# Two more buffers for split weights, five units kept for the second tile, and an aligned start of the large buffers

## The chip, the cores and the metric

The kernel runs on one core of one Trainium2 chip. The time is the device time of one execution in microseconds (us). The engines are TensorE (PE in the profile; its loads of the stationary operand are PEld), VectorE (DVE), ScalarE (ACT), GpSimd (POOL) and SyncE (SP), which issues the transfers of weights.

## The reference, cut to what matters

Two transformer blocks follow one another on 256 rows of 1024 float32 numbers. The first has a block attention and a gated delta rule, a gated merge, an output product, a gated feed-forward layer of width 2816 and a small embedding with a gate. The second has a differential attention, pooling, an output product, cross attention over a memory of 256 rows, and a feed-forward layer. After each large product the row is normalised, added to the residual and normalised again before the next product:

```
h = h + rms_norm(merged @ w_out, ln_post_mix)
f = rms_norm(h, ln_pre_ffn)
f = (silu(f @ w_ffn_gate) * (f @ w_ffn_up)) @ w_ffn_down
h = h + rms_norm(f, ln_post_ffn)
h = h + sigmoid(h @ w_ple_gate) * rms_norm(p @ w_ple, ln_ple)
...
x = x + rms_norm(mix @ w_out_2, g_mix_post)
xq = rms_norm(x, g_x_pre) @ w_xq
x = x + rms_norm(softmax(xq k') v @ w_xo, g_x_post)
x = x + rms_norm(ffn(rms_norm(x, g_ffn_pre)), g_ffn_post)
```

## The kernel before, in words

**Weights.** All weights are cut into 294 units of 128 x 1024 numbers (`UNITS`), in the order in which TensorE uses them. Each unit goes through three stages in this order: SyncE brings it into one of `RAW` = 4 raw slots; ScalarE rounds it to the high part `w_hi` (L1213, one copy of 128x1024); GpSimd computes the low part `w_lo` = raw - high (L470, two halves). High and low part stand in slot n % `SPLIT` of `SPLIT` = 6. A raw slot is free when the low part of its unit is there; a split slot is free when TensorE has counted the unit in `w_used`. A product with the split activations (`uH`, `uL` and others) is a triple of matmuls (`split_mm`, L481 to L483): high by high, high by low, low by high. The activation is the stationary operand and the weights move past it, except in `conv` (L829 to L831) and `keys` (L740 to L742), where the weights are stationary and 256 columns of activations move.

**Queues.** Each engine runs one list of instructions in order. ScalarE's list mixes the copies of weights with the work of the stages: `split_up_to(n)` emits the copies of all units below n at that place, and each waits for its transfer and for the release of its slot. `split_past(step, j)` is `split_up_to(NUMBER[step, j] + 1 + SPLIT)`, so its last copy waits for the release of unit j of that step. Whatever ScalarE has behind such a copy waits with it.

**Row products.** `proj_b`, `w_out`, `ple_gate`, `xq` and `xo` have eight units each and are written by `skewed_rows`, `out2` and `down` by `row_unit` and `row_tail`. A unit has four pieces (row tile t = 0 or 1, column half c = 0 or 1), each one triple into its own PSUM bank `L[2t+c]`. Row tile 0 runs ahead of tile 1: the last `TAIL` = 4 units are first used for tile 0 and then for tile 1, so that the normalisation of tile 0 runs beside the last pieces of tile 1. In `skewed_rows` the units 2 and 3 of tile 1 stand before the last three units of tile 0.

**Between two products** (ScalarE `norm` and `next`, the same on VectorE): ScalarE sums the squares of a bank (`row_sum`, L1300); VectorE multiplies by a gain (L1835), takes the root (seven small operations, L1768), adds the residual (L1853) and scales (`hg`, L1864); TensorE turns four blocks (`turn_half`, L686); ScalarE rounds them to `uH` (`hi_half`, L1225); VectorE computes `uL` (L1801). This goes by quarters, (t, half) = (0,0), (0,1), (1,0), (1,1). `following` puts the turn of (0,0) before the very last piece of a product. VectorE's list has `uL` of quarter (0,1) ahead of the root and sum for tile 1. ScalarE's has two copies of weights between the quarters (0,1) and (1,0), and the sum of squares of the whole row tile 1 (`square_sum`, L1289) before `uH` of (1,1).

**Column products** after such a junction (`ffn` 0 of both blocks and `in2` 0 and 1) are written by `skewed_columns`: for tile 0 four units of the first matrix and two of the second, then the same six units for tile 1, then the last two units of the second for both tiles. For tile 1 the third unit waits for `uL` of quarter (1,1).

**Cross attention.** ScalarE copies the last values to `xv` (`values_out`, L1244) after `split_past(("xkv", 3), 3)`, and TensorE's `cross_values` (L804) reads them.

**Memory.** The buffers are placed one after another from `base`. `w_hi`, `w_lo`, `uH` and `uL` start at multiples of 512 bytes from `base`; `Y`, where `yH`, `yL`, `hH` and `hL` stand, starts at such a multiple plus 32, and so do `B` = Y + 16 KB and all that is placed from it (`mH`, `mL`, `pH` and the buffers of attention and norms).

Of the kernel before, what the change touches and what calls it, by code (L numbers as in the profile page):

```python
# [22 lines left out]
F32 = mybir.dt.float32  # L23
F32R = mybir.dt.float32r
# [22 lines left out]
RAW, SPLIT = 4, 6  # L47
UNIT = 1024
KB = 1024
MAGIC = 1.5 * 2.0 ** 23  # L50
# [109 lines left out]
HEAD = 5  # L160
TAIL = 4

# [56 lines left out]
def build(nc, a, out, known):  # L219
# [7 lines left out]
    for n, (step, j, _) in enumerate(UNITS):  # L227
        FIRST.setdefault(step, n)
        LAST[step] = n
        NUMBER[step, j] = n  # L230
    ctx = ExitStack()
    with ctx:
# [101 lines left out]
        cp = big("cp", 16, [P, NT, GH, SEQ])  # L334
        cpT = place("cpT", [P, NT, GH, SEQ], F32, Y)
        used = B + 100 * KB
        assert used <= nc.sbuf_usable_end, (used, nc.sbuf_usable_end)
# [126 lines left out]
        @block.gpsimd  # L464
        def _(pool):
            for n in range(len(UNITS)):
                pool.wait_ge(w_hi_there, n + 1)
                for half in range(2):
                    cc = slice(half * UNIT // 2, (half + 1) * UNIT // 2)
                    last = nc.gpsimd.tensor_tensor(w_lo[:, n % SPLIT, cc], raw[:, n % RAW, cc], w_hi[:, n % SPLIT, cc].bitcast(F32),  # L470
                                                   ALU.subtract)
                last.then_inc(w_lo_there, 1)
# [3 lines left out]
        def _(pe):  # L476
# [8 lines left out]
            def unit(n, k):  # L485
                slot = n % SPLIT
                return (w_hi[:, slot, :].rearrange("p (k n) -> p k n", k=k),
                        w_lo[:, slot, :].rearrange("p (k n) -> p k n", k=k))

            def column_unit(step, j, banks, n=512, sH=uH, sL=uL, tiles=range(NT), ks=None):  # L490

# [19 lines left out]
                if 1 in tiles and per - 1 in ks:  # L511
                    last.then_inc(w_used, 1)
                elif 1 not in tiles and k == k_tiles - 1:
                    last.then_inc(*PE.mark(step, "first tile"))
# [60 lines left out]
            def skewed_rows(step):  # L575
# [38 lines left out]
            def skewed_columns(first, second, first_banks, second_banks):  # L614


                source = INPUT[first[0]]
                for t in range(NT):
                    wait_low(source, t, 0)
                    bank_free(source, t, 0)  # L620
                    for j in range(4):
                        if j == 1:
                            turn_half(source, t, 1)
                        elif j == 2:
                            wait_low(source, t, 1)
                        column_unit(first[0], first[1] + j, first_banks, tiles=(t,))
                    bank_free(source, t, 1)
                    for j in range(2):
                        if t == 0 and j == 1:
                            turn_half(source, 1, 0)  # L630
                        column_unit(second[0], second[1] + j, second_banks, tiles=(t,))
                for j in range(2, 4):
                    column_unit(second[0], second[1] + j, second_banks)
# [55 lines left out]
            def wait_low(source, t, half):  # L689

                pe.wait_ge(*VE(source, "lo", t, half))
# [152 lines left out]
            for step in SCHEDULE:  # L844
# [328 lines left out]
                elif kind == "dnorm":  # L1173
# [7 lines left out]
                    pe.wait_ge(*AC(("xkv", 1), 1))  # L1181
                    for j in range(4):
                        row_unit(("out2",), j, uH, uL, KD)
# [18 lines left out]
        def _(act):  # L1202
# [24 lines left out]
            def split_past(step, j):  # L1227


                split_up_to(NUMBER[step, j] + 1 + SPLIT)  # L1230

# [105 lines left out]
            def fill(step, i):  # L1337

                split_up_to(FIRST[FILLING[step][0]] + i + SPLIT)

# [4 lines left out]
            for step in SCHEDULE:  # L1345
# [3 lines left out]
                if kind in ("ba", "rates", "tri", "conv", "decay", "moba", "tok", "feat", "within", "att", "inv", "scan", "z", "ga", "gb"):  # L1349
                    split_up_to(consumed + SPLIT - 1)  # L1350
                if kind == "u":
# [16 lines left out]
                elif kind == "rates":  # L1368
                    split_up_to(consumed + SPLIT + 1)
                    act.wait_ge(*VE(step, "ba"))  # L1370
# [156 lines left out]
                elif kind == "down":  # L1527
                    prev = ("ffn", step[1], 5)
                    if step[1] == 1:
                        split_past(step, 2)  # L1530
                        act.wait_ge(landed["lnm"], 16)
                        for j in range(4):
# [20 lines left out]
                elif kind == "norm":  # L1553
# [6 lines left out]
                    if what == "ffn2":  # L1560
                        row_sum(what, 2)
                        row_sum(what, 3)
                        continue
                    split_past(src_step, last - 3)
                    if pre:
                        kept(what, 0, 0)
                elif kind == "next":
# [15 lines left out]
                    if pre:  # L1583
                        kept(what, 1, 1)
                        square_sum(what, 1)
                    hi_half(step, 1, 1)
                elif kind == "ffn":
                    _, blk, c = step
                    n = 512 if c < 5 else 256
                    half = (LAST[step] + 1 - FIRST[step]) // 2  # L1590
                    split_up_to(FIRST[step] + half + SPLIT - 1)
                    act.wait_ge(*fed(step, half))
# [11 lines left out]
                    for c_ in todo:  # L1604
                        prev = ("ffn", blk, c_)
                        if c_ == 5:
                            split_up_to(FIRST[("down", blk)] + SPLIT)
                        elif (blk, c) == (1, 1):
# [11 lines left out]
                    split_up_to(consumed + SPLIT - 1)  # L1620
                elif kind == "in2":
# [724 lines left out]
```

## Time and profile before

| | |
|---|---|
| median of 3 runs | 1018.12 us (1018.11 to 1018.43) |
| profiled execution | 1018.06 us, span of the instructions 1016.2 us |
| TensorE busy | 982.5 us (97%), granted clock 1.0 of full speed in every slice |
| GpSimd busy | 741.5 us (73%), 588 halves of low parts, 1300 ns each |
| ScalarE busy | 513.1 us (50%), 304.9 us of it the 294 copies of weights |
| VectorE busy | 366.5 us (36%) |
| DMA | 165 GB/s in the mean |

TensorE is nearly always busy, so the profile is read in two ways: how far apart matmuls of one shape start, and where TensorE has an idle gap and what ended it. Busy times of matmuls overlap (one starts while the one before drains), so the distance of two starts is the cost, not the busy time.

### The profile page before, as it was taken

Reading aid. Unit: us, or ns where it says so; the run is one execution under the profiler, and the core shown is the slowest. Engines: PE = TensorE matmul, PEld = TensorE weight load, DVE = VectorE, ACT = ScalarE, POOL = GpSimd, SP = SyncE. Lnnn points to the kernel's source line nnn. Section 1 sums busy time; section 2 is a strip of 40 time slices with the busy share of each in tenths; the row PEclk is TensorE's granted clock in tenths of the full one; section 3 lists DMA queues with packets and bytes.
Section 4 is the critical chain, followed back from the end, with each engine's and each line's share of the span. In section 5 each row is a group of like instructions: output and inputs, shape, how many; then the busy total and the mean of one; then the engine's idle time right before and its main releaser. Section 6 shows DMA issues by size and latency. Waiting matters only on the chain.

```text
span 1016.2 us, 15323 instructions
## 1 busy us (share of the span) xinstructions
PE 982.5 (97%) x6004; PEld 826.8 (81%) x6004; DVE 366.5 (36%) x840; ACT 513.1 (50%) x759; POOL 741.5 (73%) x592
## 2 busy tenths in 40 slices
PE   5999999999999998999999998999989999999997
PEld 5988889988888876888898876899868868888885
DVE  4677524686524135112122244243242161111103
ACT  5476624464524435465454455485465365444431
POOL 6767643877633876989986966878767469988891
PEclk9999999999999999999999999999999999999999
DMA  8546232554423665667764645655555247766551
GB/s 263 175 133 194 90 120 64 167 159 152 126 85 103 212 202 166 207 202 208 208 186 145 197 149 172 240 167 168 164 170 162 83 144 228 207 188 188 185 166 41
DMA packets 76752, 167.37 MB, mean 165 GB/s; under 512 B 8348, under 2 KB 13704, under 8 KB 76552
## 3 DMA queue, kind: packets, MB, share of 16 engines
q1 hardware_dynamic: 71296, 156.40, 49.9%
q10 hardware_dynamic: 5384, 9.99, 3.0%
q8 instruction: 47, 0.77, 0.3%
q14 instruction: 25, 0.20, 0.1%
HBM read 165.32 MB, written 1.05 MB: 164 GB/s over the span
## 4 chain that ended last, share of the span: by engine, by line
PE 86%; DVE 4%; ACT 4%; POOL 3%; issue 2%; DMA 0%; DVEq 0%; ACTq 0%
PE L L481 20%; PE L L483 19%; PE L L482 19%; POOL w_lo L470 3%; PE L L829 2%; PE L L830 2%; PE L L831 2%; PE Q L481 2%; PE Q L483 2%; PE Q L482 2%; PE Q L998 1%; ACT w_hi L1213 1%; PE Q L980 1%; PE Q L686 1%; ACT uH L1225 1%
## 5 line engine op out<-in xcount | busy, mean ns | idle before, releaser
L470 POOL TENSOR_TENSOR w_lo<-raw,w_hi 128x512 fp32r<-128x512 f32 x588 | 741.3, 1300 | 254.1 <-ACT w_hi L1213 253.5
L1213 ACT CAST w_hi<-raw 128x1024 fp32r<-128x1024 f32 x294 | 304.9, 1054 | 262.4 <-PE L L483 118.8
L481 PE MATMUL L<-w_hi,uH 128*128 128x512 f32 (+1 forms) x768 | 306.9, 400 | 12.8 <-POOL w_lo L470 4.8
L483 PE MATMUL L<-w_hi,uL 128*128 128x512 f32 (+1 forms) x768 | 296.5, 386 | 0.0
L482 PE MATMUL L<-w_lo,uH 128*128 128x512 f32 (+1 forms) x768 | 296.1, 386 | 0.0
L481 PEld LDWEIGHTS L<-w_hi,uH 128*128 128x128 f32 x768 | 144.4, 188 | 52.2 <-DVE uL L1801 9.9
L483 PEld LDWEIGHTS L<-w_hi,uL 128*128 128x128 f32 x768 | 144.3, 188 | 29.8
L482 PEld LDWEIGHTS L<-w_lo,uH 128*128 128x128 f32 x768 | 144.6, 188 | 26.1 <-issue 0.5
L481 PE MATMUL L<-w_hi,hH 128*128 128x512 f32 x176 | 70.0, 398 | 0.0
L482 PE MATMUL L<-w_lo,hH 128*128 128x512 f32 x176 | 69.6, 395 | 0.0
L483 PE MATMUL L<-w_hi,hL 128*128 128x512 f32 x176 | 69.6, 395 | 0.0
L1762 DVE TENSOR_TENSOR hL<-Q,hH 128x512 fp32r<-128x512 f32 x22 | 15.2, 692 | 121.3 <-ACT hH L1619 120.8
L829 PE MATMUL L<-uH,w_hi 128*128 128x256 f32 x192 | 55.5, 289 | 0.0
L830 PE MATMUL L<-uL,w_hi 128*128 128x256 f32 x192 | 54.9, 286 | 0.0
L831 PE MATMUL L<-uH,w_lo 128*128 128x256 f32 x192 | 54.8, 286 | 0.0
L1835 DVE TENSOR_TENSOR L<-L,gA 128x512 f32<-128x512 f32 x20 | 14.0, 700 | 103.5 <-ACT hg L1300 103.0
L1768 DVE TENSOR_SCALAR small<-small 128x1 f32<-128x1 f32 (+1 forms) x177 | 39.0, 220 | 24.3 <-ACT xv L1544 13.4
L1801 DVE TENSOR_TENSOR uL<-Q,uH 128x512 fp32r<-128x512 f32 x28 | 19.3, 691 | 58.4 <-ACT uH L1225 58.4
L483 PEld LDWEIGHTS L<-w_hi,hL 128*128 128x128 f32 x176 | 33.1, 188 | 8.0
L482 PEld LDWEIGHTS L<-w_lo,hH 128*128 128x128 f32 x176 | 33.1, 188 | 7.7
L481 PEld LDWEIGHTS L<-w_hi,hH 128*128 128x128 f32 x176 | 33.1, 188 | 7.7
L1771 DVE SCALAR_TENSOR_TENSOR hm<-L,small,sil 128x512 f32<-128x512 f32 x20 | 15.0, 751 | 66.6 <-PE L L483 66.2
(335 smaller groups left out, 1283.2 us busy)
## 6 DMA issues: line engine op xcount, KB each, us to landing
raw<-in_w_in SPq DMA_DIRECT2D x88, 512.0 KB, 3.6
raw<-in_w_ffn_gate SPq DMA_DIRECT2D x22, 512.0 KB, 3.6
raw<-in_w_ffn_up SPq DMA_DIRECT2D x22, 512.0 KB, 3.7
raw<-in_w_ffn_down SPq DMA_DIRECT2D x22, 512.0 KB, 3.5
raw<-in_w_gate SPq DMA_DIRECT2D x22, 512.0 KB, 4.2
raw<-in_w_up SPq DMA_DIRECT2D x22, 512.0 KB, 4.1
raw<-in_w_down SPq DMA_DIRECT2D x22, 512.0 KB, 3.5
raw<-in_w_out SPq DMA_DIRECT2D x16, 512.0 KB, 3.6
```

The source lines that it names most:

```text
L470: last = nc.gpsimd.tensor_tensor(w_lo[:, n % SPLIT, cc], raw[:, n % RAW, cc], w_hi[:, n % SPLIT, cc].bitcast(F32), ALU.subtract)
L481: mm(dst, sH, wH, start=start, stop=False)
L482: mm(dst, sH, wL, start=False, stop=False)
L483: return mm(dst, sL, wH, start=False, stop=stop)
L829: mm(bank, sH, uH[:, k, :], start=k == 0, stop=False)
L830: mm(bank, sH, uL[:, k, :], start=False, stop=False)
L831: last = mm(bank, sL, uH[:, k, :], start=False, stop=k == KD - 1)
L1213: copy(w_hi[:, u % SPLIT, :], raw[:, u % RAW, :]).then_inc(w_hi_there, 1)
L1762: v(V.tensor_tensor(out_, x_, y_, op), *name)
L1768: v(V.tensor_scalar(out_, x_, s1, s2_, op0, op1), *name)
L1771: v(V.scalar_tensor_tensor(out=out_, in0=x_, scalar=s_, in1=y_, op0=op0, op1=op1), *name)
L1801: vector_next(V.tensor_tensor(uL[:, 4 * half:4 * half + 4, t * P:(t + 1) * P], heads(Q[2 * t + half]), uH[:, 4 * half:4 * half + 4, t * P: ...
```

## The change

(a) Six further slots of split weights lie in memory that is free for a time; two of them are open in each of four stretches (`SCAN`: from unit 7 of `proj_a` to `ffn` 1,4; `GATE`: from unit 19 of `down` 1 to `in2` 2; `OUT`: from unit 6 of `out2` to `ffn` 2,0; `MEMORY`: from unit 4 of `xo` to the end). `SLOT` and `BEFORE` say for each unit its slot and the unit that had it before; the copy waits for `w_used` of that one. `room(used)` is the number of units that may be split once `used` units are used: 8 ahead in the stretches, up to 10 around `xo`, 6 elsewhere. All `split_*` calls use it in place of `+ SPLIT`.
(b) `TAIL` is 5: unit 3 of a row product (unit 17 of `down`) is held for tile 1 too. In `skewed_rows` only unit 2 of tile 1 stands in the middle.
(c) In `skewed_rows` the turn of quarter (0,1) stands after the third piece and not after the first.
(d) `skewed_columns` takes for tile 1 two units of the first matrix, two of the second, and then the last two of the first; the wait for quarter (1,1) stands before these.
(e) ScalarE makes `uH` of (1,1) before `square_sum` of tile 1.
(f) `Y` starts at a multiple of 512 bytes from `base`.

```diff
-TAIL = 4
+TAIL = 5
+    LENT = {SPLIT: (SCAN, MEMORY), SPLIT + 1: (SCAN, MEMORY), SPLIT + 2: (GATE,), SPLIT + 3: (GATE,), SPLIT + 4: (OUT,), SPLIT + 5: (OUT,)}
...
+        slot = min(free_slots, key=lambda s: newest.get(s, -1))
+        SLOT.append(slot)
+        BEFORE.append(newest.get(slot, -1))
...
+    def room(used):
+        n = 0
+        while n < len(UNITS) and BEFORE[n] < used:
+            n += 1
+        return n
...
+        at[0] += (base - at[0]) % SPAN
         Y = at[0]
...
-                    if j == 0 and source[0] == "next":
+                    if j == 2 and source[0] == "next":
                         turn_half(source, 0, 1)
...
-                for j in (2, 3):
+                for j in range(2, KD - TAIL):
...
+                wait_low(source, 1, 0)
+                bank_free(source, 1, 0)
+                column_unit(first[0], first[1], first_banks, tiles=(1,))
+                turn_half(source, 1, 1)
+                column_unit(first[0], first[1] + 1, first_banks, tiles=(1,))
+                bank_free(source, 1, 1)
+                for j in range(2):
+                    column_unit(second[0], second[1] + j, second_banks, tiles=(1,), used=0)
+                wait_low(source, 1, 1)
+                column_unit(first[0], first[1] + 2, first_banks, tiles=(1,))
+                column_unit(first[0], first[1] + 3, first_banks, tiles=(1,), used=3)
...
-                    if u >= SPLIT:
-                        act.wait_ge(w_used, u - SPLIT + 1)
-                    copy(w_hi[:, u % SPLIT, :], raw[:, u % RAW, :]).then_inc(w_hi_there, 1)
+                    if BEFORE[u] >= 0:
+                        act.wait_ge(w_used, BEFORE[u] + 1)
...
+                    copy(halves[SLOT[u]][0], raw[:, u % RAW, :]).then_inc(w_hi_there, 1)
...
-                split_up_to(NUMBER[step, j] + 1 + SPLIT)
+                split_up_to(room(NUMBER[step, j] + 1))
...
-                    split_past(src_step, last - 3)
+                    split_past(src_step, last - TAIL + 1)
...
+                    hi_half(step, 1, 1)
+                    if pre:
                         square_sum(what, 1)
-                    hi_half(step, 1, 1)
```

The calls `split_past(step, 3)` in `w_out`, `ple_gate`, `out2`, `xq` and `xo` are as before.

## Rows read from the trace of the kernel before

**Rows 1.** Page, part 1: busy us (share of the span) x instructions.
```profile
PE 982.5 (97%) x6004; PEld 826.8 (81%) x6004; DVE 366.5 (36%) x840; ACT 513.1 (50%) x759; POOL 741.5 (73%) x592
```

**Rows 2.** Waits of PE, whole span: waiter, releaser: us in total, times, longest.
```profile
PE L L481 <- POOL w_lo L470: 4.8, 11, 0.8
PE L L481 <- DVE uL L1801: 4.2, 6, 0.8
...
PE L L481 <- DVE small L1768: 2.6, 3, 1.0
```

**Rows 3.** Timeline of PE in `ffn` 2,2: start us, duration, instruction.
```profile
879.69 0.39 PE L482 MATMUL L<-w_lo,uH 128*128 128x512 f32 x1
...
885.58 0.39 PE L481 MATMUL L<-w_hi,uH 128*128 128x512 f32 x1
```

**Rows 4.** Timeline of PE in `down` 2.
```profile
959.72 0.40 PE L481 MATMUL L<-w_hi,hH 128*128 128x512 f32 x1
...
965.55 0.40 PE L482 MATMUL L<-w_lo,hH 128*128 128x512 f32 x1
```

**Rows 5.** Groups by line and form, PE: xcount | busy us, mean ns | idle before.
```profile
L481 PE MATMUL L<-w_hi,hH 128*128 128x512 f32 x176 | 70.0, 398 | 0.0
...
L481 PE MATMUL Q<-w_hi,mH 128*128 128x512 f32 x32 | 13.1, 409 | 0.0
L481 PE MATMUL L<-w_hi,yH 128*128 128x512 f32 x32 | 12.9, 403 | 0.0
```

**Rows 6.** Timeline of PE in the first `conv`.
```profile
17.54 0.28 PE L829 MATMUL L<-uH,w_hi 128*128 128x256 f32 x1
...
19.94 0.28 PE L831 MATMUL L<-uH,w_lo 128*128 128x256 f32 x1
```

**Rows 7.** Timeline of PE in `keys` of the memory.
```profile
674.72 0.28 PE L741 MATMUL L<-mL,w_hi 128*128 128x256 f32 x1
...
677.76 0.28 PE L740 MATMUL L<-mH,w_hi 128*128 128x256 f32 x1
```

**Rows 8.** Timeline of PE, end of `w_out`; in brackets idle before and its releaser.
```profile
381.51 0.40 PE L483 MATMUL L<-w_hi,uL 128*128 128x512 f32 x1
382.72 0.50 PE L481 MATMUL L<-w_hi,uH 128*128 128x512 f32 x1 [0.82 <-POOL w_lo L470]
...
388.98 0.60 PE L686 MATMUL Q<-table,hg 128*128 128x128 f32 x4
...
391.05 0.50 PE L481 MATMUL L<-w_hi,uH 128*128 128x512 f32 x1 [0.78 <-DVE uL L1801]
```

**Rows 9.** Timeline of ACT, end of `w_out`.
```profile
376.52 3.89 ACT L1213 CAST w_hi<-raw 128x1024 fp32r<-128x1024 f32 x4
383.72 0.60 ACT L1300 ACTIVATE hg<-L 128x512 f32<-128x512 f32 x1 [3.31 <-PE L L483]
```

**Rows 10.** Timeline of DVE, end of `w_out`.
```profile
387.87 0.69 DVE L1864 TENSOR_TENSOR hg<-L,gB 128x512 f32<-128x512 f32 x1
```

**Rows 11.** Timeline of POOL in `w_out`.
```profile
377.65 8.77 POOL L470 TENSOR_TENSOR w_lo<-raw,w_hi 128x512 fp32r<-128x512 f32 x7 [6.17 <-ACT w_hi L1213]
```

**Rows 12.** Timeline of ACT and of PE in `ffn` 1,0, tile 1.
```profile
403.50 1.06 ACT L1289 ACTIVATE tmp<-h 128x1024 f32<-128x1024 f32 x1
...
405.98 0.50 PE L481 MATMUL L<-w_hi,uH 128*128 128x512 f32 x1 [0.78 <-DVE small L1768]
```

**Rows 13.** Timeline of DVE in `ple_gate`.
```profile
593.34 0.69 DVE L1801 TENSOR_TENSOR uL<-Q,uH 128x512 fp32r<-128x512 f32 x1 [0.79 <-ACT uH L1225]
...
595.75 0.75 DVE L1853 SCALAR_TENSOR_TENSOR h<-L,small,h 128x512 f32<-128x512 f32 x1
```

**Rows 14.** Timeline of ACT and of PE in the cross attention.
```profile
786.59 1.07 ACT L1244 COPY xv<-Q 128x512 f32<-128x512 f32 x2
...
787.71 2.05 PE L804 MATMUL Q<-cpT,xv 128*128 128x128 f32 x16 [0.38 <-ACT xv L1244]
```

**Rows 15.** DMA issues by line: KB each, median us to landing.
```profile
gB<-in_g_mix_pre ACTq DMA_DIRECT2D x1, 512.0 KB, 3.7
```

More of the change, by code:

```diff
@@ L48 @@
 UNIT = 1024
+SPAN = 512
 KB = 1024
@@ L230, in build @@
         NUMBER[step, j] = n
+    SCAN, GATE, OUT, MEMORY = range(4)
+    OPENED = {SCAN: NUMBER[("proj_a",), 7], GATE: NUMBER[("down", 1), 19], OUT: NUMBER[("out2",), 6], MEMORY: NUMBER[("xo",), 4]}
+    CLOSED = {SCAN: LAST["ffn", 1, 4], GATE: LAST["in2", 2], OUT: LAST["ffn", 2, 0], MEMORY: len(UNITS) - 1}
+    LENT = {SPLIT: (SCAN, MEMORY), SPLIT + 1: (SCAN, MEMORY), SPLIT + 2: (GATE,), SPLIT + 3: (GATE,), SPLIT + 4: (OUT,), SPLIT + 5: (OUT,)}
+    SLOT, BEFORE = [], []
+    newest = {}
+    for n in range(len(UNITS)):
+        if n == OPENED[MEMORY]:
+            newest.update({s: LAST["xkv", 3] for s, whens in LENT.items() if MEMORY in whens})
+        free_slots = list(range(SPLIT)) + [s for s, whens in LENT.items() if any(OPENED[o] <= n <= CLOSED[o] for o in whens)]
+        slot = min(free_slots, key=lambda s: newest.get(s, -1))
+        SLOT.append(slot)
+        BEFORE.append(newest.get(slot, -1))
+        newest[slot] = n
+    ENTRY = {n: o for o in (SCAN, GATE, OUT) for n in [next(n for n in range(OPENED[o], len(UNITS)) if SLOT[n] >= SPLIT)]}
+    def room(used):
[3 more added lines that the diff above has]
+        return n
     ctx = ExitStack()
@@ L335, in build @@
         cpT = place("cpT", [P, NT, GH, SEQ], F32, Y)
+        lent = {SPLIT: (84, 88), SPLIT + 1: (92, 96), SPLIT + 2: (68, 72), SPLIT + 3: (76, 80), SPLIT + 4: (60, 64), SPLIT + 5: (-8, -4)}
+        halves = {n: (w_hi[:, n, :], w_lo[:, n, :]) for n in range(SPLIT)}
+        for n, (hi_at, lo_at) in lent.items():
+            halves[n] = (big(f"w_hi{n}", hi_at, [P, UNIT], F32R)[:], big(f"w_lo{n}", lo_at, [P, UNIT], F32R)[:])
         used = B + 100 * KB
@@ L469, in _ @@
                     cc = slice(half * UNIT // 2, (half + 1) * UNIT // 2)
-                    last = nc.gpsimd.tensor_tensor(w_lo[:, n % SPLIT, cc], raw[:, n % RAW, cc], w_hi[:, n % SPLIT, cc].bitcast(F32),
-                                                   ALU.subtract)
+                    hi, lo = halves[SLOT[n]]
+                    last = nc.gpsimd.tensor_tensor(lo[:, cc], raw[:, n % RAW, cc], hi[:, cc].bitcast(F32), ALU.subtract)
                 last.then_inc(w_lo_there, 1)
@@ L485, in unit, with column_unit @@
             def unit(n, k):
[L486 to L490, printed above, removed]
+                hi, lo = halves[SLOT[n]]
+                return hi.rearrange("p (k n) -> p k n", k=k), lo.rearrange("p (k n) -> p k n", k=k)
+            def column_unit(step, j, banks, n=512, sH=uH, sL=uL, tiles=range(NT), ks=None, used=1):
                 n0 = NUMBER[step, j]
@@ L511, in column_unit @@
                 if 1 in tiles and per - 1 in ks:
-                    last.then_inc(w_used, 1)
+                    if used:
+                        last.then_inc(w_used, used)
                 elif 1 not in tiles and k == k_tiles - 1:
@@ L617, in skewed_columns @@
                 source = INPUT[first[0]]
[L618 to L631, printed above, removed]
+                wait_low(source, 0, 0)
+                bank_free(source, 0, 0)
+                for j in range(4):
+                    if j == 1:
+                        turn_half(source, 0, 1)
+                    elif j == 2:
+                        wait_low(source, 0, 1)
+                    column_unit(first[0], first[1] + j, first_banks, tiles=(0,))
+                bank_free(source, 0, 1)
+                column_unit(second[0], second[1], second_banks, tiles=(0,))
+                turn_half(source, 1, 0)
+                column_unit(second[0], second[1] + 1, second_banks, tiles=(0,))
+                wait_low(source, 1, 0)
[9 more added lines that the diff above has]
+                column_unit(first[0], first[1] + 3, first_banks, tiles=(1,), used=3)
                 for j in range(2, 4):
@@ L1181, in _ @@
                     pe.wait_ge(*AC(("xkv", 1), 1))
-                    for j in range(4):
+                    for j in range(KD - TAIL):
                         row_unit(("out2",), j, uH, uL, KD)
@@ L1337, in fill @@
             def fill(step, i):
-                split_up_to(FIRST[FILLING[step][0]] + i + SPLIT)
+                split_up_to(room(FIRST[FILLING[step][0]] + i))
             load("ident", table[:, 0:P], a["table"][:, 0:P])
@@ L1590, in _ @@
                     half = (LAST[step] + 1 - FIRST[step]) // 2
-                    split_up_to(FIRST[step] + half + SPLIT - 1)
+                    split_up_to(room(FIRST[step] + half) - 1)
                     act.wait_ge(*fed(step, half))
```

17 lines of the change are left out of this document (13 added, 4 removed).

## The prediction, made before the change was run

> **What bounds the kernel now.** I read the page first: TensorE is busy for 982.5 of 1016.2 us [rows 1]. So a change can win only by fewer or closer matmuls, or by closing gaps, and the waits view puts the gaps inside the program at some 12 us [rows 2]: low parts of weights that come late, `uL` that comes late, and three waits that carry the name of a small VectorE operation. Then I read timelines of TensorE for the distance of starts. In `ffn` a triple's matmuls start 5.89 us / 26 = 226.5 ns apart [rows 3]; in `down` they start 5.83 / 25 = 233.2 ns apart [rows 4]. Both move 512 columns of the same weight buffers at full clock; the stationary operand is `uH`/`uL` in one and `hH`/`hL` in the other, and only the second stands at a multiple of 512 bytes plus 32. The 6.7 ns are invisible in the busy shares. Last I laid the lists of ScalarE, VectorE and TensorE beside each other at each junction of two products, since that is where all remaining gaps are.
>
> **(f) Aligned start.** 176 + 32 + 32 = 240 triples have their stationary operand in `hH`, `mH` or `yH` and their low parts [rows 5], 720 matmuls. If the start sets the distance: 720 x 6.5 ns (a little under 6.7, since after each pause some matmuls of the aligned kind run slow too) = -4.7 us. Where the buffer is the moving one it is the other way round: `keys` with `mH` has 3.04 / 26 = 116.9 ns [rows 7], `conv` with the aligned `uH` 2.40 / 20 = 120 ns [rows 6]. `keys` has 192 such matmuls: +0.6. Net -4.1. Bounds: 0 if it isn't the address, -4.7 if `keys` keeps its pace. I take -4.1, since `uH` and `hH` have the same layout and the same weights, and differ in nothing else that I can find.
>
> Here a rule speaks against the step. The Trainium skill (TensorE: Matmul & The Clock Gate, "Wait — 56ns, not 53.3ns?" and "Step-by-step: what each phase is for") gives 2.4 GHz matmuls a distance of N / 2.4 GHz + about 2.5 ns, 215.7 ns at 512 columns, and says that loading the next weights takes no read bandwidth from the running matmul; an address has no part in it. This trace shows neither that distance nor one distance. By the rule the step gives nothing.
>
> **(a) Slots.** Before, `w_out`'s unit 6 may be split only when unit 0 is used by tile 1, and ScalarE then is late: GpSimd idles 6.17 us [rows 11] and TensorE pays for units 6 and 7. A gap shows as 0.82 in brackets, but the starts 381.51 and 382.72 are 1.21 apart instead of 0.23 [rows 8]: each wait costs its idle time and about 0.16 more for restarting. All waits for low parts: 4.8 + 11 x 0.16 = 6.6 us [rows 2]. With eight slots GpSimd, which needs 2.5 us a unit (8.77 for 3.5 units [rows 11]) against 2.72 for a unit's twelve matmuls, doesn't idle there, and units 6 and 7 are ready 8 us ahead. One of these waits, in `in2`, is passed on to the turn of quarter (1,1), which hangs on a chain from the turn before it: -6.6 + 0.5 = -6.1. In steady `ffn` and `down` there are no gaps, so more slots give nothing there. The first copy into a lent slot also waits until its memory is free; in all four stretches that event lies ahead of the copy's place in ScalarE's list, so it costs nothing.
>
> **(d), (e) Last half.** Three column starts wait for `uL` (1,1) [rows 2, 12]: 2.6 + 3 x 0.16 = -3.1. It goes: two units of 1.36 us stand before the wait now, and the square sum (1.06, [rows 12]) has left the way. The next candidate, `kept` of (1,1), is 0.6 after `hg`, beside a unit of 1.36. The other 4.2 us of `uL` waits [rows 2] stay: the turn before the last piece leaves only 0.7 us of cover for a chain of 1.7 (388.98 to 391.05 [rows 8]).
>
> **(b) with `split_past(step, 3)`: a new wait.** This is the cost I weigh most. The last copy at that call is for the unit whose slot unit 3 has (u = 99 in `w_out`, `BEFORE` 91). Unit 3 was used up before tile 0's end; with `TAIL` = 5 it is used up by the first two pieces of tile 1's tail. ScalarE has `row_sum` of tile 0 behind this copy. From the end of bank 0 the wait is three pieces of 0.68 = 2.04, 0.25 to see it, and a copy of 0.97 (3.89 / 4 [rows 9]): `row_sum` starts 3.3 us after bank 0, 3.1 later than now. From its start to the end of `hg` are 4.84 us (383.72 [rows 9] to 388.56 [rows 10]). TensorE needs the turn 10 x 0.68 = 6.8 after bank 0; it gets it 3.3 + 4.84 = 8.15 to 8.2 after. That is +1.4 us in `w_out`, `out2` and `xo` each, though the longer tail alone would have given 1.36 more slack (0.4 now [rows 8, 10]). In `ple_gate` the load of the gain `gB` stands behind the same copy; it needs 3.7 us [rows 15], then three VectorE operations of 0.7: 2.3 + 3.9 + 2.2 = 8.4 after bank 0, +1.65. Behind the copies in `xq` and `proj_b` nothing is due so early. Sum +5.85. Bounds: 0 if the order hides it, +9 if each copy also waits for a late transfer.
>
> **(c) Turn of (0,1) later.** It moves by two pieces, 1.36 us, and VectorE has the root and sum of tile 1 behind that `uL` (593.34 to 595.75 and its 0.75, [rows 13]). In `ple_gate` the sum is then ready 3.16 after `uL`'s start, 0.7 us after TensorE wants the turn of (1,0): +0.7. In `xq` the turn waited 0.4 us anyhow, so it moves by 0.75; that delay runs through the same chain, and a third copy of weights on ScalarE between (0,1) and (1,0) adds 0.2: +0.95. Together +1.65, the saved wait counted. Bounds 0 and +2.6.
>
> **Cross attention.** `split_past(("xkv", 3), 3)` may go to unit 229 here. After `xkv` 3 ends there are three copies (227 to 229) before `values_out`, where one stood. Two more at 0.97: `xv` at 789.6 instead of 787.66, and TensorE waits for it already [rows 14]: +1.95. Bounds: 0 and +4 if the transfer of 229 lands late.
>
> **Sum.** -4.1 - 6.1 - 3.1 + 5.85 + 1.65 + 1.95 = -3.85. The profiled execution took 1018.06 us (span 1016.2 and 1.9 around it), within 0.1 of the median of the runs, so the time is 1018.1 - 3.9 = **1014.2 us**.
>
> **Rivals.**
> 1. *ScalarE isn't held* (a longer slack at the junctions than I see, or the held copies come in time): the 5.85 go. 1014.2 - 5.85 = 1008.4. For it: ScalarE is half idle [rows 1]. Against: its list is strictly in order and the wait for unit 3 is a matter of piece order. Chance 0.15.
> 2. *The address has no part*: `down` keeps 233 ns and `keys` 117 because of something else about the operands. Then 1014.2 + 4.1 = 1018.3, no change. (The rule of the Trainium skill named above would have it so.) For it: the operands in the upper buffers also differ in region; against: 233.2 and 226.5 with one layout. Chance 0.2.
> 3. *Slower.* The held copies on ScalarE's list, priced at their upper bounds: each of the four held copies has a transfer to wait for too, because raw slots come free only with the low parts and these now run four units deep; then +9 for 5.85 and +4 for 1.95, and `keys` and float32 products lose from the alignment what `down` wins (another 1 to 2 us). 1014.2 + 3.15 + 2.05 + 1.5 = 1020.9. It decides from the point where new waits (9.5 in my sum) exceed 13.3. For it: two more copies stand before each due operation; against: the transfers land in about 3.6 us and GpSimd is not behind at these places. Chance 0.13.
> 4. *The change doesn't do what it says*: the slots open too late to serve, so that the low-part waits stay while the new waits come. 1014.2 + 5 = 1019, counted with 3 in the chances (0.03).
>
> **How the numbers follow.** Forecast 0.49, own range 1012.2 to 1016.2 (the sums of half the bounds); rivals as above. A change of 0.2%, 2 us, is about what can be told from none here: faster means below 1016.1, slower above 1020.2. Faster: 0.47 of the forecast, 0.15 of rival 1, 0.05 of rival 2: 0.67. Slower: 0.12 of rivals 3 and 4 and 0.01 of rival 2: 0.13. Same: 0.20. The range 1008.2 to 1019.0 holds the forecast, rival 2 and the upper half of rival 1; the rest of rival 1 and most of rival 3 are left out, together under 0.2.
>
> **What would show it.** Starts in `down`: 226.5 ns right, 233 wrong for (f); `keys` 120. The 11 waits for low parts should be gone. At the end of `w_out`, `out2` and `xo` a new idle gap before the turn of `hg`, ended by VectorE, of about 1.2 us, and on ScalarE a copy of weights between the last pieces of tile 0 and the first square sum; none of it would make rival 1 right. In `ple_gate` and `xq` a gap before the turn of (1,0). In the cross attention 2.3 us before the second `cross_values`. The prediction is wrong if the sum of these new gaps is under 5 or over 13 us, or if `down` keeps its pace.

## The result, and the profile after

The change made the kernel slower: 1023.89 us median (1022.10 to 1024.95, 4 runs) against 1018.23 (1018.11 to 1018.43), ratio 1.0055 [1.0042, 1.0067]. The forecast was 1014.2. The profiled execution took 1022.10, the least of the four; the mean granted clock of the four was 0.994, 0.992, 0.989 and 0.991, where the recorded executions of the kernel before, in all sessions, had 0.997 to 0.999. (The table of the kernel before has the first three of these four runs, hence its 1018.12.)

The page of the kernel after, first line and part 1, against [rows 1]: TensorE is busy 2.4 us less than before, in a span that is 4.1 us longer.

```profile
span 1020.3 us, 15320 instructions
...
PE 980.1 (96%) x6004; PEld 829.9 (81%) x6004; DVE 366.2 (36%) x840; ACT 510.5 (50%) x759; POOL 741.6 (73%) x592
```

The waits of PE after (waiter, releaser: us in total, times, longest), against [rows 2]: the low parts and the small operation are gone from the list. `hg` and `xv` have grown from 0.8 and 0.4 in all, `gs` and `cqT` are new, and single waits reach 3.3 us where before no wait for an engine inside the products was over 1.0.

```profile
PE Q L725 <- DVE hg L1913: 7.7, 6, 3.3
...
PE L L511 <- DVE uL L1850: 3.6, 6, 0.8
PE L L511 <- DVE gs L2146: 2.5, 1, 2.5
PE Q L843 <- ACT xv L1291: 2.3, 1, 2.3
PE L L818 <- ACT cqT L1305: 1.2, 1, 1.2
```

The timeline of PE in `down` 2, against [rows 4]: 34 distances in 7.71 us, 226.8 ns each and no longer 233.2.

```profile
957.65 0.39 PE L511 MATMUL L<-w_hi,hH 128*128 128x512 f32 x1
...
965.36 0.39 PE L512 MATMUL L<-w_lo,hH 128*128 128x512 f32 x1
```

**The end of `w_out`.** First ScalarE: the copy at 385.11 waited for a matmul (the release of unit 3) and `row_sum` stands behind it. Then TensorE: the turn comes 1.18 us late, and 0.78 is lost again before the last piece, as in [rows 8].

```profile
385.11 1.05 ACT L1260 CAST w_hi<-raw 128x1024 fp32r<-128x1024 f32 x1 [3.48 <-PE L L513]
386.06 0.59 ACT L1347 ACTIVATE hg<-L 128x512 f32<-128x512 f32 x1
```

```profile
390.95 0.66 PE L725 MATMUL Q<-table,hg 128*128 128x128 f32 x4 [1.18 <-DVE hg L1913]
...
393.08 0.52 PE L511 MATMUL L<-w_hi,uH 128*128 128x512 f32 x1 [0.78 <-DVE uL L1850]
...
393.83 0.63 PE L513 MATMUL L<-w_hi,uL 128*128 128x512 f32 x1
394.25 0.63 PE L511 MATMUL L<-w_hi,uH 128*128 128x512 f32 x1
394.68 0.63 PE L512 MATMUL L<-w_lo,uH 128*128 128x512 f32 x1
```

The last three starts are 0.43 us apart where the same matmuls stand 0.227 apart elsewhere. The windows view after tells why (stretch: length, busy time and count of PE, PEld, DVE, ACT and POOL, granted clock, DMA share, GB/s). In the trace before the granted clock is 1.00 from 17.4 us to 1014.1.

```profile
389.40:393.40 4.00, 2.04 (x10) 1.18 (x9) 3.21 (x5) 2.34 (x6) 2.93 (x3) 1.00 0.72 228
393.40:396.80 3.40, 3.40 (x11) 2.71 (x10) 1.68 (x3) 0.17 (x1) 0.00 (x0) 0.50 0.49 152
396.80:401.00 4.20, 4.20 (x19) 3.22 (x18) 3.40 (x10) 4.20 (x6) 2.28 (x2) 1.00 0.00 0
...
614.60:618.70 4.10, 0.82 (x7) 0.42 (x5) 2.09 (x3) 0.57 (x2) 2.94 (x3) 1.00 0.99 332
618.70:622.10 3.40, 3.21 (x10) 2.10 (x8) 2.26 (x4) 1.80 (x4) 0.00 (x0) 0.50 0.65 237
788.00:792.80 4.80, 2.53 (x20) 2.23 (x18) 0.00 (x0) 4.07 (x6) 4.61 (x5) 1.00 0.58 193
792.80:796.20 3.40, 3.40 (x16) 3.40 (x17) 0.69 (x1) 0.33 (x1) 3.40 (x4) 0.50 0.68 167
```

Three times the clock fell from 2.4 to 1.2 GHz, each time right after idle gaps of TensorE (1.18 and 0.78; 3.27; 2.27), and each time for 3.4 us. The same pair of gaps, 1.18 and 0.78, stands at the ends of `out2` and `xo` too, and the 2.46 at `proj_b`, with no fall behind them.

**`ple_gate`.** ScalarE's queue issues the load of `gB` at 610.36, when the held copy starts. By the view of DMA issues it lands 5.6 us later, not 3.7 [rows 15], while the DMA engines are 92 to 99% busy. VectorE, then TensorE, wait for it (timelines of ACT, DVE, PE after):

```profile
610.34 1.05 ACT L1260 CAST w_hi<-raw 128x1024 fp32r<-128x1024 f32 x1 [2.39 <-PE L L513]
610.36 0.34 ACTq L1357 DMA_DIRECT2D gB<-in_g_mix_pre  x1
```

```profile
616.07 0.70 DVE L1906 TENSOR_TENSOR L<-L,e 128x512 f32<-128x512 f32 x1 [11.26 <-DMA gB<-in_g_mix_pre]
```

```profile
618.28 0.76 PE L725 MATMUL Q<-table,hg 128*128 128x128 f32 x4 [3.27 <-DVE hg L1913]
```

**`proj_b`.** I had given this place nothing. ScalarE's list after has a copy before each `hi_half` of `yb`, and each copy waits for a transfer:

```profile
333.57 1.05 ACT L1260 CAST w_hi<-raw 128x1024 fp32r<-128x1024 f32 x1 [1.15 <-DMA raw<-in_w_proj_b]
334.52 0.58 ACT L1272 CAST uH<-Q 128x512 fp32r<-128x512 f32 x1
335.79 1.05 ACT L1260 CAST w_hi<-raw 128x1024 fp32r<-128x1024 f32 x1 [0.69 <-DMA raw<-in_w_proj_b]
336.74 0.58 ACT L1272 CAST uH<-Q 128x512 fp32r<-128x512 f32 x1
338.40 1.05 ACT L1260 CAST w_hi<-raw 128x1024 fp32r<-128x1024 f32 x1 [1.08 <-DMA raw<-in_w_proj_b]
```

The first `hi_half` ran at 328.94 before and at 334.52 after, the fourth at 341.68 instead of 336.85. TensorE then waits; the wait is put down to `gs`, the last of VectorE's work behind the fourth `uL`:

```profile
343.75 0.47 PE L511 MATMUL L<-w_hi,uH 128*128 128x512 f32 x1 [2.46 <-DVE gs L2146]
```

The copies are 2.2 to 2.6 us apart because a raw slot comes free only with a low part: SyncE's own waits here are for `w_lo`, and GpSimd computes 18 halves in 22.49 us without a pause, 2.5 us a unit. A copy two units further ahead has room in the split slots, but no data.

**A measure for what follows.** Between 20 and 1005 us I add up, for all matmuls, the distance to the next start beyond the usual one of the shape (226.5 ns, 120 ns and so on): the *gap sum*, apart for stretches at full and at half clock. It holds over 30 us that no kernel here touches; its differences count. No view of the profile has it: how the shapes are grouped moves a sum by up to 1 us, and so does to which side a gap at the edge of a slow stretch is counted, so differences under 1 us say little. Before: 42.5 at full clock and 0 at half. After: 44.6 and 5.4.

### The profile page after: what moved, and what is told of

Read it like the earlier page. It is cut to its first block, busy times and chain, and to the rows that moved or that the text cites. A ratio compares the mean times of both kernels' runs of the same rounds, so it can differ in the third digit from the quotient of the medians.

```text
span 1020.3 us, 15320 instructions
## 1 busy us (share of the span) xinstructions
PE 980.1 (96%) x6004; PEld 829.9 (81%) x6004; DVE 366.2 (36%) x840; ACT 510.5 (50%) x759; POOL 741.6 (73%) x592
## 4 chain that ended last, share of the span: by engine, by line
PE 84%; DVE 6%; ACT 4%; DMA 3%; POOL 2%; issue 2%; SPq 0%; DVEq 0%; ACTq 0%
PE L L511 19%; PE L L513 18%; PE L L512 18%; PE L L868 2%; PE Q L513 2%; PE Q L511 2%; PE Q L512 2%; PE L L870 2%; PE L L869 2%; POOL w_lo L501 2%; ACT w_hi L1260 2%; PE Q L1037 1%; PE Q L725 1%; PE Q L1019 1%; DMA raw<-in_w_in 1%
```

## The experiments

Each is timed beside the kernel before on its own chip: 1, 3, 4 and 5 on one, 6, 7, 8 and 14 on a second, 9 to 12 on a third, 2, 13 and 15 on a fourth. The kernel before has medians of 1018.09, 1017.97, 1018.10 and 1018.12 there, so times may be compared across them to about 0.15 us. "Gaps" gives the gap sum at full / half clock of the profiled execution. The next four build the change up.

**1. Alignment alone**, the kernel before with

```diff
+        at[0] += (base - at[0]) % 512
         Y = at[0]
```

> The kernel before with part (f) alone (Y at a multiple of 512 bytes). Theory A (the start of the stationary operand sets the distance of starts, as my term has it): down at 226.5 ns, keys at 120 ns, -4.1 us, 1014.1. Rival B (float32 matmuls and attention, whose buffers move with Y too, lose what down wins): the same 226.5 ns in down, but 1016 to 1018. The granted clock stays 1.0 under both.

Measured: 1014.25 (1014.08 to 1014.34), ratio 0.9962 [0.9950, 0.9975]; gaps 42.4 / 0. In `down`, as in all below:

```profile
950.32 0.39 PE L482 MATMUL L<-w_hi,hH 128*128 128x512 f32 x1
...
952.36 0.39 PE L482 MATMUL L<-w_hi,hH 128*128 128x512 f32 x1
```

Nine distances in 2.04 us. In `keys` 18 take 2.15 us (672.24 to 674.39), 119.4 ns where it was 116.9. Theory A holds: 3.8 us from one line, and the runs lie within 0.3 us of each other.

**2. Slots alone**, (f) and (a): the changed kernel with (b) to (e) undone.

```diff
-TAIL = 5
+TAIL = 4
...
-                    if j == 2 and source[0] == "next":
+                    if j == 0 and source[0] == "next":
```

and the bodies of `skewed_columns` and the end of `next` as before.

> Parts (f) and (a) alone. (The kernel I ran as (f) and (a) had kept (d)'s order of skewed_columns, against what its expectation says; here it is undone.) My terms for (d) and (e): 3.1 more than that kernel where the clock doesn't fall, 1011.2 against 1008.0 of span and so 1013.0, with falls 1013 to 1016. Rival: once the slots bring the low parts in time, the three waits for uL of (1,1) are gone without (d), 1010 to 1011.5.

Measured: 1015.86 (1013.66 to 1017.39), ratio 0.9976 [0.9965, 0.9988]; gaps 41.3 / 3.0. So the slots by themselves *cost* 1.6 us against experiment 1: idle time is a little less, and the clock costs more than that. Its waits of PE:

```profile
PE L L511 <- DVE uL L1841: 5.7, 6, 1.9
...
PE L L511 <- DVE small L1808: 3.0, 3, 1.0
PE L L511 <- DVE gs L2137: 2.5, 1, 2.5
PE Q L834 <- ACT xv L1282: 2.3, 1, 2.3
```

The 11 waits for low parts are gone, as I had it. But `proj_b` (2.5), the start of `in2` (1.9 where it was 0.8) and `cross_values` (2.3) came with the slots, and the clock fell twice. The rival is wrong: the waits for the last half stay.

**3. Slots and (d).** Its expectation speaks of (f) and (a) alone, but the kernel has (d) too; number 2 is the one without. Against number 2:

```diff
+                for j in range(2):
+                    column_unit(second[0], second[1] + j, second_banks, tiles=(1,), used=0)
+                wait_low(source, 1, 1)
```

> Parts (f) and (a) only: TAIL 4, old order of skewed_columns, old place of the turn of (0,1), square_sum first. Theory A (my terms, to which the trace after adds two delays by copies that ScalarE may now make too early: proj_b's start +2.4, the second half of the cross queries +1.4): 1014.1 - 6.1 (low-part waits) + 1.95 + 2.4 + 1.4 = 1013.8. Theory C (a long idle gap also lowers TensorE's clock): the gap of about 2.3 us at the second cross_values is followed by a stretch at 0.5, +1.5: 1015.3. Rival D (the delay at proj_b and in the cross attention belongs to the longer tail, not to the slots): 1010.

Measured: 1011.39 (1010.29 to 1013.41), ratio 0.9935 [0.9923, 0.9947]; gaps 37.1 / 3.4. The three waits named after `small` are gone: (d) works, 4.2 of gap sum. By its own terms, less 3.1 for (d), theory A gives 1010.7 and theory C 1012.2; the median lies between and the clock did fall, twice, though at `proj_b` and `ple_gate` and not at `cross_values`, where theory C had it. Its clock, in the windows view, after the gap at `proj_b`:

```profile
339.00:343.90 4.90, 1.99 (x9) 1.36 (x9) 2.49 (x4) 2.57 (x4) 4.90 (x5) 1.00 0.69 212
343.90:347.30 3.40, 3.40 (x10) 2.63 (x9) 1.28 (x3) 1.40 (x2) 3.40 (x4) 0.50 0.45 167
```

**4. Slots, (d) and (e).**

```diff
+                    hi_half(step, 1, 1)
                     if pre:
                         square_sum(what, 1)
-                    hi_half(step, 1, 1)
```

> As the kernel with (f) and (a), and (d) and (e) too. My term: 3.1 less than that kernel (the three waits for uL of (1,1) gone), so 1010.7 by theory A and 1012.2 by theory C. Rival: the waits are passed on to the next piece and less than 1 us comes of it.

Measured: 1010.86 (1009.97 to 1014.64), ratio 0.9934 [0.9922, 0.9946]; gaps 38.4 / 4.6. No difference from number 3 that these runs can tell: (e) gains nothing to be seen once (d) is there. From 2 to 4 the gap sum fell by 2.9, and my term for (d) and (e) together was 3.1. The six runs say more: those at 0.998 of the clock took 1009.97 and 1010.06, the one at 0.993 took 1014.64.

**5. And (b)**: the changed kernel with (c) undone.

```diff
-TAIL = 4
+TAIL = 5
```

> The changed kernel with part (c) undone, so the step from the kernel with (f), (a), (d), (e) to this one is (b) alone. Theory A (gaps count at their length): +5.85, 1016.5. Theory C (the gaps of 1.9 us at the end of w_out and of 3.3 us in ple_gate each start a stretch of about 3.4 us at 0.5 of the clock, in some executions those of out2 and xo too): +9 to +12, 1021 to 1023. If the ple_gate gap falls below 3 us without (c), one stretch less.

Measured: 1022.39 (1019.87 to 1023.21), ratio 1.0037 [1.0025, 1.0049]; gaps 44.2 / 5.1. (b) adds 5.8 us of gap sum at full clock; I had forecast 5.85. The time rose by 11.5. Theory C, as expected. The places don't match the forecast as well as the sum does: the wait for `cqT` (1.57 idle) came with (b) and wasn't in the term, and the waits for `uL` fell from 5.7 to 3.6.

**6. The hold taken out**, that is the copy that waits for unit 3 while due work stands behind it. In the changed kernel, at the start of `w_out`, `ple_gate`, `out2`, `xq` and `xo`:

```diff
-                    split_past(step, 3)
+                    split_past(step, KD - TAIL - 1)
```

> The changed kernel, with the copies at the start of w_out, ple_gate, out2, xq and xo going only as far as the release of unit 2 and not of unit 3, so none waits for tile 1. Theory A (ScalarE is held by that copy, my new wait): the gaps before the turn of hg in w_out, out2, xo (1.14 each) and most of the 3.3 in ple_gate go, 1023.9 - 3.4 - 2.5 = 1018, and with the stretches at half clock that followed them, 1015 to 1016. Rival D (the copies behind transfers, paced by GpSimd at 2.5 us a unit, hold ScalarE and not the release of unit 3): the gaps stay and the time is within 1 us of 1023.9.

Measured: 1011.11 (1009.56 to 1012.64), ratio 0.9933 [0.9920, 0.9945]; gaps 38.6 / 0. Waits of PE:

```profile
PE L L511 <- DVE uL L1850: 4.2, 6, 0.8
...
PE L L511 <- DVE gs L2146: 3.3, 1, 3.3
PE Q L843 <- ACT xv L1291: 2.3, 1, 2.3
PE Q L725 <- DVE hg L1913: 1.3, 3, 0.5
```

The waits for `hg` fall from 7.7 to 1.3 and that for `cqT` is gone: 12.8 us from one number at five places, more than theory A said (6 to 9). The theory is right on the cause and rival D falls. The runs again go with the clock: 1009.56 at 0.999, 1012.43 and 1012.64 at 0.994 and 0.995.

**7 and 8. Every copy at its old place in the list**: `split_past` is capped at six units ahead, in the changed kernel (7) and in that of experiment 4 (8).

```diff
-                split_up_to(room(NUMBER[step, j] + 1))
+                split_up_to(min(room(NUMBER[step, j] + 1), NUMBER[step, j] + 1 + SPLIT))
```

> The changed kernel, but each copy stands where a lag of six units puts it in ScalarE's list (the number of copies at split_past is capped at 6 ahead); slots, TAIL 5 and all else as changed. Theory A': both kinds of delay (release of unit 3, and transfers that land at GpSimd's pace) come from copies placed earlier in the list: the gaps at proj_b (2.4), w_out, out2, xo (1.1 each), ple_gate (3.3), the cross queries (1.4) and cross_values (1.9) go, 12 us, and the falls of the clock with them: 1005 to 1009, if the low parts stay in time. Rival E (the slots help only because of the earlier places): the low-part waits return, up to 6.1: 1011 to 1014.

> The same cap in the kernel with TAIL 4, (a), (d), (e), (f). Theory A': its gaps at proj_b (2.7) and cross_values (1.9) and 1 us in ple_gate go, 1010.9 - 5.6 = 1005, less its falls of the clock (0 to 3 in its runs, 1.6 each): 1003 to 1005. Rival E: low-part waits return, 1008 to 1011. Against the same with TAIL 5 it tells what the fifth held unit is worth once ScalarE isn't held: 3 x 0.4 us in favour of TAIL 5 by the waits for hg before, nothing otherwise.

Measured: 1039.01 (1037.51 to 1039.81), ratio 1.0205 [1.0191, 1.0219], gaps 61.3 / 6.8; and 1014.94 (1012.96 to 1015.46), ratio 0.9965 [0.9953, 0.9977], gaps 41.8 / 1.6. Theory A' is wrong. The gaps at the junctions and in the cross attention went, and the low parts are late. First the line of 7, then that of 8:

```profile
PE L L511 <- POOL w_lo L501: 25.1, 17, 4.7
```

```profile
PE L L511 <- POOL w_lo L501: 5.7, 10, 1.1
```

The earlier places in the list are needed, most of all with `TAIL` 5, and slots without them give nothing (8 is no faster than experiment 1). The gap at `proj_b` stayed (2.7), since the copies there come from `fill` and weren't capped; number 9 does that.

**9. The copies in `yb` at six units ahead**, added to number 6.

```diff
-                        fill(step, i)
+                        split_up_to(FIRST["proj_a",] + i + SPLIT)
```

> The kernel with the held copies taken back to unit 2 (1011.11, 1009.6 where the clock didn't fall), and the copies inside yb kept six units ahead, so that copy 81 to 84 stand behind the hi_half's again. Theory A (the copies that the slots allow earlier wait for transfers that land 2.5 us apart, and hi_half waits with them): the gap of 3.3 us at the start of proj_b goes, and with it the fall of the clock that follows it in some executions: 1006 to 1007. Rival: the low parts of proj_b are late instead (they start later by nothing, since GpSimd sets the pace), 1009 to 1010.

Measured: 1008.20 (1006.36 to 1009.74), ratio 0.9900 [0.9885, 0.9916]; gaps 36.4 / 1.7. The wait for `gs` is gone from the list. 2.9 us less than number 6, at a place where I had written that nothing was due. Theory A said 1006 to 1007: the two runs at 0.998 of the clock took 1006.36 and 1006.99, and the profiled one had a fall behind the 2.27 us of the cross attention.

**10. And the cross attention**, added to number 9:

```diff
-                    split_past(values, 3)
                     values_out(3, [Q[2], Q[3]])
+                    split_past(values, 3)
```

> The same, and in the cross attention the copies of split_past(values, 3) stand behind values_out. The gap before the second cross_values goes from 2.27 to under 0.4, 1.9 less, and the falls of the clock behind it: 1004 to 1005. Rival: the copies are late for xo's first units instead, no gain.

Measured: 1006.68 (1006.02 to 1007.28), ratio 0.9886 [0.9871, 0.9901]; gaps 34.8 / 0. Half a miss: the wait for `xv` went, and a wait for `uL` before the first piece of `xo` came, because `cross_hi` now stood behind the copies.

```profile
PE L L511 <- DVE uL L2364: 1.8, 1, 1.8
```

**11. (c) undone** in number 10 (first edit), and **12. `TAIL` 4** in number 10 (second).

```diff
-                    if j == 2 and source[0] == "next":
+                    if j == 0 and source[0] == "next":
...
-TAIL = 5
+TAIL = 4
```

> The same as the kernel with both, with (c) undone (the turn of (0,1) after the first piece). My term for (c) was +1.65, so 1.6 less: 1002.5 to 1003.5. Rival: with ScalarE no longer held the turn hides in both places and nothing changes; the traces show 0.50 of wait for h in ple_gate with (c) and none without.

> The same as the kernel with both, with TAIL 4. If the fifth held unit is worth its slack at the junctions (waits for hg of 0.4 us in w_out, out2 and xo, three times): 1.2 more than with TAIL 5. If nothing hangs on it: within 0.5.

Measured: 11: **1004.91** (1004.72 to 1006.15), ratio 0.9871 [0.9856, 0.9886], gaps 34.6 / 0. 12: 1008.35 (1007.28 to 1010.33), ratio 0.9899 [0.9882, 0.9915], gaps 37.1 / 1.5. So the fifth held unit is worth about 2 us (1.7 by the medians, 2.3 by the gap sums) once it holds nobody up. For (c) the medians differ by 1.8. The traces differ by 0.2 us of gap sum, with spans of 1004.3 both, but the profiled execution of 11 was the longest of its four, by 1.1 us. It holds waits that have nothing to do with (c): 1.06 for `uL` at 365 us, where 10 has 0.60, and 0.66 at 649 with no releaser. Place by place 10 has two waits for `h` that 11 lacks, 0.51 in `ple_gate` and 0.46 in `xq`, and `hg` waits 0.49 in place of 0.43; with about 0.16 for each restart (c) costs 1.3 us, by estimate from these rows. Number 11 is the fastest of all, 13 us below the kernel before and 19 below the changed one. The first of the two waits for `h`, in the waits of 10:

```profile
PE Q L725 <- DVE h L1902: 0.5, 1, 0.5
```

**13. Only one copy before the values**, the others behind `cross_hi`, in number 11.

```diff
+                    split_up_to(NUMBER[values, 3] + 1 + SPLIT)
                     values_out(3, [Q[2], Q[3]])
-                    split_past(values, 3)
                     cross_hi(0)
                     cross_probs(1)
                     cross_hi(1)
+                    split_past(values, 3)
```

> The best kernel so far (1004.91), with only one copy of weights before values_out and the others behind cross_hi. Theory (copies of weights placed ahead of due work make that work late, wherever they stand): the wait of 1.8 us for uL at the start of xo, which took the place of the one before cross_values, goes and nothing takes its place: 1003.0 to 1003.5. Rival: the two copies are then late for xo's last units, low-part waits of 1 to 2 us: 1004 to 1005.

Measured: 1008.13 (1007.76 to 1008.46), ratio 0.9901 [0.9887, 0.9914]; gaps 34.4 / 2.8. A miss. Both waits of the cross attention are gone, and the next due work is late in their place (timeline of ACT, end of `xo`'s tile 0):

```profile
789.08 3.89 ACT L1260 CAST w_hi<-raw 128x1024 fp32r<-128x1024 f32 x4
796.30 1.05 ACT L1260 CAST w_hi<-raw 128x1024 fp32r<-128x1024 f32 x1 [3.32 <-DMA raw<-in_w_gate]
798.82 1.05 ACT L1260 CAST w_hi<-raw 128x1024 fp32r<-128x1024 f32 x1 [1.47 <-DMA raw<-in_w_gate]
801.35 1.05 ACT L1260 CAST w_hi<-raw 128x1024 fp32r<-128x1024 f32 x1 [1.48 <-DMA raw<-in_w_up]
802.31 0.59 ACT L1347 ACTIVATE hg<-L 128x512 f32<-128x512 f32 x1
```

```profile
PE Q L725 <- DVE hg L1914: 4.2, 4, 3.0
```

The copies are 2.5 us apart, at the pace of transfers, and `row_sum` waits behind the third. Number 11 has them at 795.23 in one stretch and `row_sum` at 800.62. Moving copies back delays GpSimd: it starts on low parts at 790.22, runs 22.4 us without a pause, and the copies behind it wait for it through the raw slots. One gap of 3.0 is worse than one of 1.8, and the clock fell for 6.8 us after it.

**14 and 15. What a gap costs.** The kernel of experiment 1, with four (14) or two (15) more copies of a bank into free memory ahead of the values of the cross attention:

```diff
+                    for i in range(4 if (t, c) == (0, 3) else 0):
+                        copy(spare[i // 2][:, i % 2, :], banks[t][:])
```

> The kernel before with (f) alone, and in the cross attention ScalarE makes four more copies of a bank into free memory before the values, 0.53 us each by the row of xv; nothing else is added. The idle gap of TensorE before cross_values grows from 0.4 to 2.5 us. If a gap costs its length: 1014.25 + 2.1 = 1016.4, granted clock 1.0 as in the kernel without it. If such a gap also lowers the clock in some executions: one stretch of 3.4 us at 0.5 after it, and single runs at 1018.

> The kernel before with (f) alone and two added copies before the values: TensorE's gap before cross_values 1.4 us where the kernel with four had 2.3. If a gap costs its length alone: 1014.25 + 1.07 = 1015.3 in each run. If a gap of this length too can lower the clock: some runs 1.5 higher, as the one with four copies (1016.1 to 1016.6 in five runs, 1017.5 to 1018.3 in six).

Measured; first the wait with two copies, then with four:

```profile
PE Q L806 <- ACT xv L1248: 1.4, 1, 1.4
```

```profile
PE Q L806 <- ACT xv L1248: 2.3, 1, 2.3
```

Two copies: 1015.21 (7 runs, 1015.12 to 1015.82), ratio 0.9972 [0.9961, 0.9983], so +0.96 for a gap 0.97 longer, and the clock at 0.998 or 0.999 in each. Four copies: 1017.52 (11 runs), in two groups with nothing between: five of 1016.09 to 1016.64 at 0.998 or 0.999, and six of 1017.52 to 1018.29 at 0.997. The first group costs the gap's length (1014.25 + 1.95 = 1016.2); the second is 1.57 above it in the mean. One stretch of 3.4 us at half clock would cost that: eight matmuls 0.427 apart in place of fifteen 0.2265 apart, 3.41 x (1 - 0.2265 / 0.427) = 1.6, and it would lower the mean clock by 0.5 x 3.41 / 1014 = 0.0017, as seen. The profiled execution (1016.30) is of the first group and has no fall, so that the second group had one is inferred from its times and mean clocks. The mean clock alone wouldn't do: the kernel before has 0.997 in some executions of unchanged time.

The Trainium skill (TensorE: Matmul & The Clock Gate, "Terms") puts the penalty at the throttled time times the share of clock withheld, 3.41 x 0.5 = 1.7 us by estimate; the 1.57 measured come near it. The section "Why this matters for your kernels" of the same page of the Trainium skill warns of idle gaps between bursts of matmuls that are longer than most of those here. These runs show falls after 2.27 us, after 1.83 (experiment 3, `ple_gate`), after 1.79 (experiment 12, where 10 and 11 had none after 1.78), and after 1.18 and 0.78 with a few matmuls between, and the measurement decides.

## Why the prediction was wrong, step by step

- **(f) aligned start: right.** -4.1 forecast, -3.8 measured alone. Rival 2 falls. The Trainium skill (TensorE: Matmul & The Clock Gate, "Wait — 56ns, not 53.3ns?") gives 215.7 ns as the distance for 512 columns; the traces here show 233.2 and 226.5, and the address decides which.
- **(a) low parts: right, but not its surroundings.** The waits went. "Behind the copies in `xq` and `proj_b` nothing is due so early" failed at both places. At `proj_b` the four `hi_half` stood behind copies that had room and no data, 2.6 us, in every kernel with the slots up to number 8. Behind `xq`'s stood the heads of the cross queries, 1.4 us; this came with `TAIL` 5 (2 to 4 don't have it) and went with the hold (6). The start of `in2` lost another 1.1 in experiment 2, where copies ahead of the due work waited 3.02 us for a transfer. I had treated a copy's wait as a wait for its slot alone; the transfer stood in my bounds and in rival 3, not in the sum.
- **(d), (e): right in sum**, 2.9 of gap sum for 3.1. It is (d) alone: 4.2 with it, and 1.3 back with (e), in one trace each.
- **(b), the hold: mechanism right; that the sum fits, 5.8 for 5.85 (4 to 5), is partly luck.** `w_out`, `out2` and `xo` are right: 1.18 idle, with 0.16 for the restart 1.34 where I had 1.4. In `ple_gate` it is 3.27 idle for a predicted cost of 1.65, as its `gB` took 5.6 us and not 3.7 to land. `cqT` (1.57) wasn't in the sum. Against these, waits for `uL` that number 4 had became shorter by 2.1 in all, and a wait for `hg` of 0.4 in `ple_gate` went.
- **(c): about right.** +1.65 forecast. The waits that it brings, 0.50 and 0.46 for `h` in the whole change as in 10, come to about 1.3. From 5 to the whole change the gap sum rose by 0.4 only, as the waits at `cqT` and `proj_b` happened to be 0.3 and 0.2 shorter; the time rose by 1.5.
- **Cross values: right.** 2.27 idle against 2.3 expected in "What would show it".
- **The step that failed** is the sentence under (a): "each wait costs its idle time and about 0.16 more for restarting". It was read from waits of at most 1.0 us and used for gaps of up to 2.3, of which one became 3.3. In some executions such a gap also halves TensorE's clock, for 3.4 us (6.8 in experiments 4, 7 and 13), up to 1.6 us for each 3.4. The slow stretch begins near the gap's end: in number 4 it began at 342.95 and the gap ended at 343.61. No term, bound or rival had it. Beside it the term for `xq` and `proj_b`, put at nothing, measured 1.4 and 2.6 us.

The miss of the profiled execution, 1022.1 - 1014.2 = 7.9, is made up so: gap sum of the stretches at half clock 5.4; gaps at full clock 2.1 where the terms beside (f) come to +0.25, so 1.9; the alignment 0.3; together 7.6. Three stretches cost at most 3 x 1.6 = 4.8, so at least 0.6 of the 5.4 is idle time that falls inside them, and idle time that I hadn't forecast is at least 2.5. Without the clock this execution would have taken about 1022.1 - 4.8 = 1017.3: above my own range of 1012.2 to 1016.2, but inside the wider one that ended at 1019.0. The three other runs had a lower mean clock than the profiled one and are 1.5 to 2.9 us longer, so that in the median run up to 4.8 + 1.8 = 6.6 of the 9.7 us are clock. That part is inferred from the mean clock, as only one execution has a trace.

Rival 3 named the right direction, and half of its mechanism (copies that wait for transfers), at 1020.9. What would have told me: the list of waits before held nothing over 1.0 us inside the products, the clock never left 1.00 there, and my own sum created seven gaps of 0.7 to 2.3 us. And the trace before does show the other state, at its ends, though the table of the kernel before says 1.0 for every slice. Up to 17.2 us, behind an idle gap of 2.59 us that ended at 11.38, the matmuls of the first `conv` start 0.21 us apart, where they stand 0.12 apart in [rows 6]; and from 1014.1, 5.6 us after the last matmul's start, the granted clock is 0.50.

```profile
16.99 0.41 PE L829 MATMUL L<-uH,w_hi 128*128 128x256 f32 x1
17.20 0.38 PE L830 MATMUL L<-uL,w_hi 128*128 128x256 f32 x1
```

Both levels of the clock stand in this trace, the lower one where TensorE is idle or has just been. The range should have been open on that side.

## What to carry to other kernels

Each wait that a change adds on an in-order queue has a length, and its price isn't linear in that: many gaps of 0.8 us were cheaper here than a few of 2 to 3, as those could take the clock down. More buffers let a producer's operations stand earlier in its queue; ask of each one not only whether its slot is free then but whether its data is there, and what is queued behind it. An operation that is held should be held behind the due work: changing 3 to 2 in five calls turned +5.7 us into -7.

## What the runs showed of the hardware

- The distance of fp32r matmuls of 512 columns depends on where the stationary operand starts: 233.2 ns at 32 bytes past a multiple of 512, 226.5 ns on it. For a moving operand of 256 columns it is the other way round, 116.9 and 119.4 ns (`keys` before and in experiment 1).
- By times and mean clocks, a gap of 1.35 us took the clock down in 0 of 7 runs and one of 2.33 us in 6 of 11, at the same place of programs that differ in two copies. In profiled executions the gap at `proj_b` was followed by a fall at 2.46, 2.66, 2.68, 2.69 and 2.91 us (experiments 2, 5, 8, 4, 3), and was not at 2.46 (after), 2.66 (7) and 3.31 (6). What decides between one execution and the next stays open.
- So kernels with such gaps scatter: 1009.97 to 1014.64 in experiment 4, while 1 stayed within 0.3 us. Here a wide spread of runs went with falls.
- A load of 512 KB on ScalarE's queue took 5.6 us where it had taken 3.7, with the DMA engines over 90% busy.
